# A ring of three PSUM banks for the turned values and forward transforms of a Fourier convolution, and one bank for the branch products

## What is computed

```python
def _hyena(u, conv_w, conv_b, kf, hyena_bias):
    L = u.shape[1]
    z = _short_conv(u, conv_w, conv_b)
    v, x1, x2 = jnp.split(z, 3, axis=-1)
    y = v.astype(jnp.float32)
    for o, gate in enumerate((x1, x2)):
        yf = jnp.fft.rfft(y, n=2 * L, axis=1)
        y = jnp.fft.irfft(yf * kf[:, o], n=2 * L, axis=1)[:, :L] + hyena_bias[o].astype(jnp.float32) * y
        y = gate.astype(jnp.float32) * y
    return y.astype(u.dtype)

def _merge(y_a, y_b, gate_logits, w_branch_a, w_branch_b, w_out):
    ga, gb = jnp.split(jax.nn.sigmoid(gate_logits), 2, axis=-1)
    return (ga * (y_a @ w_branch_a) + gb * (y_b @ w_branch_b)) @ w_out
```

## Time and profile before

| | us |
|---|---|
| median of three runs (lowest, highest) | 2128.58 (2127.46, 2130.02) |
| the profiled execution, its own time | 2127.93 |
| its span from first to last instruction | 2126.1 |
| convolve, from the first forward transform to the last gating | 677.2 to 831.6 |
| merge, to the last of the routing | to about 1018 |
| experts | to the end |

### The profile page before, as it was taken

How to read it: one execution, slowest core, us unless ns; L and a number is a source line. 1 busy time by engine, 2 the same in 40 slices (tenths; PEclk the granted TensorE clock), 3 DMA queues, 4 the chain that set the end, 5 groups by cost and what they waited for, 6 DMA issues and landing times.

```text
span 2126.1 us, 28064 instructions
## 1 busy us (share of the span) xinstructions
PE 2088.5 (98%) x10361; PEld 1688.2 (79%) x10361; DVE 1679.9 (79%) x1790; ACT 1205.6 (57%) x1321; POOL 225.8 (11%) x94
## 2 busy tenths in 40 slices
PE   8999999989999999999999999999999999999998
PEld 6988888866679785787688888888888888888886
DVE  4577765158885998855998988889988988889987
ACT  4521222256622332334487787777777787877875
POOL 2000000000000001200620222102220220102200
PEclk9999999999999999999999999999999999999999
DMA  9145454130012226443899999999999999999993
GB/s 331 35 128 167 136 187 153 50 130 16 16 50 109 89 80 241 143 179 105 326 400 409 401 401 401 391 399 379 379 375 400 388 378 379 381 402 382 378 381 114
DMA packets 189643, 541.69 MB, mean 255 GB/s; under 512 B 16877, under 2 KB 67407, under 8 KB 188928
## 3 DMA queue, kind: packets, MB, share of 16 engines
q1 hardware_dynamic: 179512, 508.92, 63.6%
q0 software_dynamic: 5264, 17.00, 3.1%
q10 hardware_dynamic: 4792, 14.74, 1.9%
HBM read 504.97 MB, written 35.66 MB: 254 GB/s over the span
## 4 chain that ended last, share of the span: by engine, by line
PE 58%; DMA 2%; SPq 1%; DVE 1%; POOL 0%; ACT 0%; issue 0%; POOLq 0%; DVEq 0%
PE p_y L346 6%; PE p_y L348 5%; PE p_y L347 5%; PE p_b L346 5%; PE p_b L347 5%; PE p_b L348 5%; PE p_a L346 5%; PE p_a L348 5%; PE p_a L347 5%; PE p_m L346 2%; PE p_m L347 2%; PE p_m L348 2%; PE p_t L3158 1%; PE p_t L3149 1%; DMA w_b<-in_w_branch_b 1%; DMA ring<-in_w_up 0%
## 5 line engine op out<-in xcount | busy, mean ns | idle before, releaser
L3025 DVE TENSOR_TENSOR r_lo<-ring,r_hi 128x2048 fp32r<-128x2048 f32 x372 | 838.7, 2286 | 57.6 <-ACT r_hi L2973 56.5
L2973 ACT ACTIVATE r_hi<-ring 128x2048 fp32r<-128x2048 f32 x372 | 708.5, 1916 | 149.5 <-PE p_b L348 72.9
L346 PE MATMUL p_y<-r_hi,a_hi 128*128 128x512 f32 x512 | 205.3, 401 | 0.0
L348 PE MATMUL p_y<-r_hi,a_lo 128*128 128x512 f32 x512 | 200.0, 391 | 0.0
L346 PE MATMUL p_a<-r_hi,x_hi 128*128 128x512 f32 x500 | 198.7, 397 | 0.6 <-POOL r_lo L2940 0.6
L347 PE MATMUL p_y<-r_lo,a_hi 128*128 128x512 f32 x512 | 199.2, 389 | 0.0
L346 PE MATMUL p_b<-r_hi,x_hi 128*128 128x512 f32 x504 | 196.7, 390 | 0.5 <-POOL r_lo L2940 0.5
L347 PE MATMUL p_b<-r_lo,x_hi 128*128 128x512 f32 x504 | 196.1, 389 | 0.0
L348 PE MATMUL p_b<-r_hi,x_lo 128*128 128x512 f32 x504 | 196.1, 389 | 0.0
L348 PE MATMUL p_a<-r_hi,x_lo 128*128 128x512 f32 x500 | 195.1, 390 | 0.0
L347 PE MATMUL p_a<-r_lo,x_hi 128*128 128x512 f32 x500 | 194.6, 389 | 0.0
(11 more groups left out here) (438 smaller groups left out, 3867.9 us busy)
## 6 DMA issues: line engine op xcount, KB each, us to landing
ring<-in_w_gate SPq DMA_DIRECT2D x128, 1024.0 KB, 10.5
ring<-in_w_up SPq DMA_DIRECT2D x128, 1024.0 KB, 9.7
ring<-in_w_down SPq DMA_DIRECT2D x128, 1024.0 KB, 12.4
ada_rest<-in_ada_w SPq DMA_DIRECT2D x16, 1024.0 KB, 5.4
w_raw<-in_w_in SPq DMA_DIRECT2D x15, 1024.0 KB, 7.4
h_parts<-in_ada_w SPq DMA_DIRECT2D x16, 512.0 KB, 9.0
gate_dram<-zs ACTq DMA_DIRECT2D x16, 512.0 KB, 2.6
x_normed<-gate_dram SPq DMA_DIRECT2D x16, 512.0 KB, 4.2
```

The lines of the kernel that those rows point to most:

```text
L346: pe.matmul(out, a_hi, b_hi, start=start, stop=False)
L348: return pe.matmul(out, a_lo, b_hi, start=False, stop=stop)
L2973: act.activation(r_hi[:, i % PARTS], ring[:, i % RAW], ACT.Copy).then_inc(hi_ready, 1)
L3025: dve.tensor_tensor(r_lo[:, i % PARTS], ring[:, i % RAW], r_hi[:, i % PARTS].bitcast(F32), ALU.subtract).then_inc(lo_ready, 1)
```

## The change

`pj` becomes three banks and `p_b` one. Bank `n` is now `pj[:, n % 3]`, and PE waits only until bank `n - 3` is empty. Each branch product waits until ACT has copied the one directly ahead of it. Bank 2 of the transposes belongs to another pair of the `spectra` stage's banks, so the wait for that pair moves from branch(0) to it. On PE, branch(0) now stands ahead of turn(1), branch(2) behind forward(2), and branch(5) ahead of back(5); on ACT the copies of branch 0 and 2 move likewise. The order of ACT and SP at the end of the stage is as it was.

```diff
-    SETS = 2 * ORD
+    SETS, BANKS = 2 * ORD, 3
...
-        pj = ps("p_j", [P, 2, 512])
-        p_b = ps("p_branch", [P, 2, 512])
+        pj = ps("p_j", [P, BANKS, 512])
+        p_b = ps("p_branch", [P, 512])
...
-                if n >= 2:
-                    pe.wait_ge(emptied, n - 1)
+                if n == BANKS - 1:
+                    pe.wait_ge(spectrum_read, S_LAST - 2)
+                if n >= BANKS:
+                    pe.wait_ge(emptied, n - BANKS + 1)
...
-                        pe.wait_ge(emptied, n - 1)
+                        pe.wait_ge(emptied, n - BANKS + 1)
...
-                if j >= 2:
-                    pe.wait_ge(branch_read, j - 1)
+                if j:
+                    pe.wait_ge(branch_read, j)
                 for c in range(NCH):
-                    mm = pe.matmul(p_b[:, j % 2], w2[:, j % 2, c, :], y2[:, c, :], start=c == 0, stop=c == NCH - 1)
+                    mm = pe.matmul(p_b[:], w2[:, j % 2, c, :], y2[:, c, :], start=c == 0, stop=c == NCH - 1)
...
             forward(1)
+            branch(0)
             turn(1)
-            pe.wait_ge(spectrum_read, S_LAST - 2)
-            branch(0)
             branch(1)
+            forward(2)
             branch(2)
-            forward(2)
             back(pe, 0)
...
             forward(7)
+            branch(5)
             back(pe, 5)
-            branch(5)
             branch(6)
...
             transformed(1)
+            branch_copy(act, 0)
             turned(1)
-            branch_copy(act, 0)
             branch_copy(act, 1)
+            transformed(2)
             branch_copy(act, 2)
-            transformed(2)
             transformed(3)
```

More of the change, by code:

```diff
@@ L2037, in turn_half @@
                         to = HC * h + P * j
-                        mm = pe.transpose(pj[:, n % 2, to:to + P],
+                        mm = pe.transpose(pj[:, n % BANKS, to:to + P],
                                           ya[:, 2 * (i % 2) + j, at:at + 4 * P - 3:4], ident[:])
@@ L2045, in turned_half @@
                 act.wait_ge(filled, n + 1)
-                act.activation(values_at(i)[:, par, q2].rearrange("p h n -> p (h n)"), pj[:, n % 2], ACT.Copy)\
+                act.activation(values_at(i)[:, par, q2].rearrange("p h n -> p (h n)"), pj[:, n % BANKS], ACT.Copy)\
                    .then_inc(emptied, 1)
@@ L2062, in forward @@
                         n = first_bank("forward", k) + 2 * odd + bank
-                        pe.wait_ge(emptied, n - 1)
+                        pe.wait_ge(emptied, n - BANKS + 1)
                         for z in range(2):
                             q = 2 * bank + 1 if odd else 2 * (bank ^ z)
-                            mm = class_sum(pe, pj[:, n % 2, HC * z:HC * z + HC], tf[:, 2 * q + z],
+                            mm = class_sum(pe, pj[:, n % BANKS, HC * z:HC * z + HC], tf[:, 2 * q + z],
                                            values_at(i)[:, odd, q // 2], c)
@@ L2115, in branch_copy @@
                 act.wait_ge(branch_stored, 16 * j)
-            act.activation(staged[:], p_b[:, j % 2], ACT.Copy).then_inc(branch_read, 1)
+            act.activation(staged[:], p_b[:], ACT.Copy).then_inc(branch_read, 1)
             act.wait_ge(branch_read, j + 1)
@@ L2132, in transformed @@
                         into = (cp, cp_other)[bank][:, odd].rearrange("p (a z n) -> p a z n", a=2, z=2)
-                        found = pj[:, n % 2].rearrange("p (z n) -> p z n", z=2)
+                        found = pj[:, n % BANKS].rearrange("p (z n) -> p z n", z=2)
                         act.activation(into[:, 0], found, ACT.Copy)
```

## The result

| | before | after |
|---|---|---|
| median, us (lowest, highest; 22 runs each, taken in turns) | 2128.84 (2126.34, 2131.23) | 2133.02 (2130.08, 2136.03) |
| the profiled execution, its own time | 2127.93 | 2132.85 |
| its span | 2126.1 | 2131.0 |

After over before is 1.0022, with a 95% interval from 1.0016 to 1.0028: the changed kernel is slower by 3.4 to 6.0 us, 4.2 between the medians. The profiled executions differ by 4.9. In the changed kernel the lines of `convolve` and of what follows it have numbers higher by one or two.

A forecast was written before the change was run, and what follows sets the result against it. DVE was taken to set the convolution's pace and PE the time from 858 us on. Delay 4.3, less 1.6 absorbed, plus 2.1 for the clock gives 4.8, on 2128.58 is 2133.3 us; range 2130.3 to 2136.0.

The forecast's parts named there:

- part 3: End of the convolution: branch(7) waits for the copy of branch 6, PE stands 6.5 us, 2.7 late after absorption.
- part 2: Convolution, branches 0, 2 and 5 moved: no effect either way, taken as zero, with thin cover at gating(2).
- the prediction's own sign: Convolution: part 2 is wrong if DVE waits for PE at gating(0), (1) or (2).
- Part 1, the ring: Start of the convolution, forward(0): a third bank lets DVE's run start and end earlier, a gain of 0.43 us.
- The term for a clock that swings through small stands at the banks: Convolution: a longer ring could win back slow matrix work; taken as zero, since the granted clock is 1.00 there.
- The first term, back(7) 4.3 late: End of the convolution: back(7) starts at 827.4 instead of 823.17, queued behind branch(7) and two merge products.
- The second, 1.6 absorbed: Merge, ahead of the first split product: PE's waits for DVE absorb 1.6 us of the delay.
- the third block's `x_normed` was to be issued at about 842.6: Merge, SP's queue: issue moves from 840.00 to about 842.6 behind the same backlog, costed at nothing.
- Part 4, the clock: branch(7) and work behind it: 4.2 us at half speed after the stand, 2.1 us lost.
- The rival in which the clock holds: Behind the stand ahead of branch(7): no low clock, only the 2.7 us delay remains, 2131.3; chance 0.17.
- The stand without cost: Merge: the chain goes through the queue of loads, not back(7); only part 1's gain remains, 2128.2; chance 0.10.
- The growing delay: Merge: back(7) 6.4 late, loads taken up in steps of one block, low clock lasts longer, 2135.8; chance 0.15.

The follow-up runs named there:

- e1: The changed kernel with ACT copying branch 6 directly behind branch 5, ahead of the four copies that wait for w_b; 2129.46 us, ratio 1.0002.
- e7: e6 with SP's two loads of the gate rows moved behind the fifth block's loads instead of the second's; 2126.37 us, ratio 0.9988.
- e3: The changed kernel with seven unused products on PE between back(6) and branch(7), filling the stand; 2132.06 us, ratio 1.0011.
- e8: The kernel before with five unused products (4.3 us) on PE between back(6) and branch(7); 2128.51 us, ratio 0.9999.
- e5: The changed kernel with SP loading w_b ahead of the last gate and the last column block; 2128.35 us, ratio 0.9999.
- e10: The changed kernel with branch 6 copied early, w_b loaded ahead of the last gate, and gate rows behind the fifth block's loads; 2129.38 against 2130.70 us, ratio 0.9994.
- e6: e1 with branch(5) put back behind back(5); 2128.41 us, ratio 0.9999.
- e2: The kernel before with one wait changed: branch(7) also waits for the copy of branch 6; 2133.64 against 2128.72 us, ratio 1.0024.
- e9: The changed kernel with two unused products on PE between branch(4) and turn(3); ran once, 2137.97 us.

## Why the prediction was right

The forecast was 2133.3, the measured median 2133.02, and the wait, its place and the low clock are in the traces as forecast. Two terms of part 3 were off by over half a microsecond each, and it is luck that they cancel; part 2 was wrong by the prediction's own sign, and what it cost is most of one of these two errors.

**Part 1, the ring: right.** 0.43 was forecast, 0.52 measured (8.75 to 8.23), in every kernel with three banks. Behind that DVE is continuous and nothing else is won. The term for a clock that swings through small stands at the banks was zero, as chosen: turn(2) of after starts behind a stand of 1.48, and the stretch around it is at the full level:

```profile
735.00:740.00 5.00, 3.70 (x24) 1.00 0.68 208
```

So here too no trace bears out what the Trainium skill describes in "TensorE: Matmul & The Clock Gate", section "A second HAM failure mode: psum-queue depth-cycling", for stands up to that length. A longer one, ahead of turn(3), did lower the clock, and that I had not looked for; it belongs to part 2.

**Part 2, the spread branches: taken as nothing, 0.74 in the profiled execution.** The prediction calls part 2 wrong if DVE waits for PE at gating(2), and it does. The two-bank kernel with the new order (e4) shows the order alone nearly free. With the ring PE is ahead of DVE by more, stands 2.11 us ahead of turn(3), and in the profiled execution the clock falls. turn(3) and forward(6) then take 10.48 instead of 8.94 in e1, where it did not fall: 1.5 us. The next product behind them, first in after and then in e1:

```profile
782.16 7.07 PE L2017 MATMUL p_acc<-idft_in,spec 128*128 128x256 f32 x32
```

```profile
780.77 7.07 PE L2017 MATMUL p_acc<-idft_in,spec 128*128 128x256 f32 x32
```

The slow stretch, with branch(5) ahead of back(5), makes DVE wait 0.43 in gating(2). Both are needed: in e1 the clock stays up and in e7 branch(5) stands behind back(5), and in neither does DVE wait there. I had written that the cover is thin, "0.1 us or some tenths", and took zero. Gating(2) ends 130.70 us after the stage's start, in e1 129.96: 0.74 lost, more than the ring's 0.52. So `w_b`, which is issued behind gating(2), is issued at 808.69 in both kernels, where the forecast had it 0.43 earlier. How often the clock falls there in executions without a profile is not known.

**Part 3, the delay: the mechanism right, two terms mis-sized.** The wait, its place, its releaser and those queued behind it are as forecast. The first term, back(7) 4.3 late, measured 4.98 in e3, where no clock is in it, and 5.09 in after: the copy of branch 6 ends at 822.72 instead of 822.2, from the later `w_b` (0.43) and 0.1 of load time, and in this execution the stage began 0.16 earlier. The second, 1.6 absorbed, measured 2.26. What was off there is "two records are one product of 0.864". The rows of these products don't give that figure: 22.58 us for 52 records is 0.868, and 0.864 is the pace of back transforms (6.91 / 8). Nor would the 0.868 have served, since a group's time holds the end of its last product, which the next one overlaps if it doesn't wait. The 30 products take 25.91 as a group, but 25.35 from their start to the start of the next (837.01 to 862.36), 0.845 each; that gives 2.15, and the remaining 0.1 is back(7), 6.91 from start to start instead of 7.01. So 4.98 - 2.26 = 2.72, where 4.3 - 1.6 gave 2.7: the errors cancelled, by luck. My expectation for e8 carried the same 1.6, and there nothing cancelled it. One more step was wrong without a price: the third block's `x_normed` was to be issued at about 842.6 behind the same backlog. In after it is issued at 845.14, 4.8 us after the backlog's end, when DVE's and ACT's late first block lets it, and DVE finds it landed.

**Part 4, the clock: right.** Forecast 4.2 us of work at half speed and 2.1 lost, measured 4.0 and 2.01. It rested on two stretches elsewhere in the kernel, and on the choice of the one followed by dense work. The rival in which the clock holds (2131.3) is what e3 makes of the kernel; its 2132.06 lies between that rival's price and the forecast, 0.8 from the one and 1.2 from the other, and in the trace the step is this one.

**The other rivals.** The stand without cost would have needed the copy of branch 6 done 2.7 us earlier. e5 and e1 do that, and give what the rival says: nothing lost, and of the gain of 0.43 nothing that runs could show. The growing delay didn't come: behind the stand PE works without a wait up to the first split product, since DVE had 4.11 of its own to give back.

## What to carry to other kernels

Before a buffer count is lowered, look up what the freeing instruction has queued in front of it on its own engine: here a copy of 0.6 us stood behind a load that it has nothing to do with, and the order of two lines on ACT decides some 4 us. A stand of an engine has three prices that are summed, not one: the delay, less what the waits behind it absorb (measured from start to start, not from the busy times of groups), plus the clock. And where a load decides, look at what its queue issues ahead of it before touching the engines.

## What the runs showed of the hardware

- A stand of 2.11 us ahead of turn(3), the same in seven traces of three-bank kernels without a fill there, was followed by a fall of the clock in five (after, e3, e5, e7, e10) and not in two (e1, e6). The instructions around it are the same in after and e1. Stands of 1.07, 1.18 and 1.48 us ahead of turns were never followed by one. What decides between the five and the two is open. Where branch(5) stands ahead of back(5) the fall reaches DVE: back(7) starts 146.14 and 146.16 after the stage's start in e5 and e10, where the clock fell, and 145.43 in e1, where it did not. In e7, with branch(5) behind, DVE does not wait, and PE is 0.47 later at back(7) than in e6.
- In the long stand the granted clock fell while PE still stood, at about 820.1 (and so in e2 and e9), so branch(7) met it low from its first record on. In attention it fell with the first product behind the stand. What a stand costs is read from the work done at the low level, not from how long the level is low: 4.0 of 6.8 us here.
- Issuing a load can take SP's queue long: 7.4 to 8.1 us for the two loads of the gate rows directly behind those of `w_out`, the router and the numbers, 0.9 behind the fifth block's two small loads (e7, e10). That it is the loads in front that make the difference is argued from these rows, not tested by itself.
- forward(0) starts within a range of 6 us in twelve executions. That is ahead of the stage; what it comes from was not looked into.
